# Mixture of experts on three lanes: the third lane starts with expert 1, and the first lane continues behind it

## The chip, the cores and the metric

One core of one Trainium2 chip runs the whole kernel. The metric is the device time of one execution in microseconds (us), the median of several runs. Engines: PE is TensorE, DVE VectorE, ACT ScalarE, POOL GpSimd, SP SyncE, which issues most of the DMAs.

## The reference

One layer over 512 tokens of 1024 channels in float32: a token mixer (not touched here), then a mixture of 16 SwiGLU experts, then a final norm. The router picks two experts of one group of four for each token.

```python
scores = sigmoid(hf @ w_router); sel = scores + router_bias
g_idx = argmax(top_k(sel by groups of 4, 2).sum(-1)); loc = top_k(in_grp, 2)
for e in range(16):
    a = silu(hf @ w_gate[e]) * (hf @ w_up[e])      # 1024 -> 512
    y = y + comb[:, e:e+1] * (a @ w_down[e])       # 512 -> 1024
```

An expert has three matrices of 2 MB each, so 6 MB.

## The kernel before

**Jobs.** Behind the mixer, PE computes the router's logits, and DVE works out the routing in a chain of small operations on tile `rt`. For every expert the tokens that chose it are cut into jobs of up to 64 tokens, at least one job for each expert. The jobs are numbered in the order of the experts: `start[e]` is the first job of expert e, `njobs` their number, and `n_rounds` = njobs/3, rounded up. DVE writes a table `jobs_i` (the expert of each place in each lane), raises `s_jb`, and a little later a table of token indices, `idx_g` and `idx_s`.

**Lanes and rounds.** A round runs three jobs, one in each lane, and each lane has its own buffer for the weights of one expert, in six chunks of 1 MB (`ew<lane>_<chunk>`: 0 and 1 gate, 2 and 3 up, 4 and 5 down). Lane 0 goes from job 0 upwards, lane 1 from the last job downwards, and lane 2 upwards from job `n_rounds`. The executed job j is that of lane j mod 3 in round j div 3. For job j PE does gate(j), up(j), the transposes of the tokens of job j+1 (`tokens`), and down(j-1), which so comes one job late. POOL gathers a job's tokens from `h2_dram` with an indirect DMA and scatters its results.

**Loads.** SP issues the loads. Expert 0 (lane 0) and expert 15 (lane 1) are loaded before the routing is known. Then SP waits for `s_xs`, `s_lg` (logits done) and `s_jb`, reads the expert of lane 2's first job from the table, and loads it. After that it runs a loop over the rounds from 1. Each turn reads six entries of the table, and issues in this order: lane 0 gate and up, lane 1 gate and up, lane 0 down, lane 2 gate and up, lane 1 down, lane 2 down. Each issue waits until the lane's last job has used that chunk (`s_gt`, `s_up`, `s_dn`). Where a lane keeps its expert, the load is still issued, but of 16 columns only (`part_` = 16, 8 KB in place of 1 MB), so that the count of the semaphore `s_er` is the same.

The counts of tokens that the reference's router gives for the 16 experts on these inputs are 43, 93, 57, 63, 195, 68, 139, 128, 5, 29, 23, 37, 30, 10, 40 and 64. That makes 1, 2, 1, 1, 4, 2, 3, 2 jobs for experts 0 to 7, one for each of the others, 24 jobs and 8 rounds. The experts by round are, before the change:

| lane | round 0 | 1 | 2 | 3 | 4 | 5 | 6 | 7 |
|---|---|---|---|---|---|---|---|---|
| 0 | 0 | 1 | 1 | 2 | 3 | 4 | 4 | 4 |
| 1 | 15 | 14 | 13 | 12 | 11 | 10 | 9 | 8 |
| 2 | 4 | 5 | 5 | 6 | 6 | 6 | 7 | 7 |

ACT, during the same stretch, writes the normed tokens to `h2_dram` with four DMAs of its own (L1022), each ahead of a copy of transposed tokens (L1016) for the logits.

Of the kernel before, what the change touches and what calls it, by code (L numbers as in the profile page):

```python
# [30 lines left out]
ALU = mybir.AluOpType  # L31
AX = mybir.AxisListType

P = 128
# [20 lines left out]
MAXR = 11  # L55
# [37 lines left out]
def trunk_kernel(nc, xT, x, cols, consts, masks, w_ada, b_ada_row, w_in, w_o_hgrn, w_o_conv,  # L93
# [15 lines left out]
    with ctx:  # L109
# [105 lines left out]
        rt = at("rt", "ON0", [P, 32, TT * NE])  # L215
# [230 lines left out]
        @block.sync  # L446
        def _(sp):
            sp.dma_start(cols_t[:, :], cols).then_inc(s_par, 16)
            sp.dma_start(con_t[:, :], consts).then_inc(s_par, 16)
            xTv = xT.rearrange("(k p) t -> p k t", p=P)  # L450
            wa = w_ada[0].rearrange("(k p) n -> p k n", p=P)

            def ada_first(b):
                for h in range(2):
                    i, c0 = 2 * b + h, D * (b % 2) + T * (b // 2)
                    sp.dma_start(ada_w[i][:, :, :], wa[:, 4 * h:4 * h + 4, c0:c0 + T]).then_inc(s_ada[i], 16)

            def chunk_load(n):
                sp.dma_start(chunk_view(w_raw, n), chunk_source(n)).then_inc(s_raw[n % 2], 16)

            for h in range(2):
                sp.dma_start(xt_t[:, 4 * h:4 * h + 4, :], xTv[:, 4 * h:4 * h + 4, :]).then_inc(s_xt[h], 16)
            ada_first(0)
            chunk_load(0)
            ada_first(1)
            chunk_load(1)
            ada_first(2)
            ada_first(3)
            sp.dma_start(mask_t[:, :], masks).then_inc(s_par2, 16)
            for n in range(NCH):  # L470
                if n >= 2:
                    sp.wait_ge(s_lo, n - 1)
                    chunk_load(n)
                if n == gn - 1:
                    sp.wait_ge(s_az, 1)
                    sp.dma_start(ada_acc[0:1, :, :].rearrange("p a n -> p (a n)"), b_ada_row).then_inc(s_ab, 16)
                if chunks[n] == ("wo", 1):
                    sp.wait_ge(s_ml, KT)
                    sp.dma_start(gffn[:, :], g_ffn.broadcast_to([P, D])).then_inc(s_gf, 16)
                if chunks[n] == ("wo", 2):  # L480
                    tile_ready(sp, at_step[("ga", 7)])
                    expert_load(sp, 0, 0, 0)
                    expert_load(sp, 0, 0, 1)
                if chunks[n] == ("wo", 0):
                    chunk_used(sp, n - 1)
                    sp.dma_start(x2_t[:, :, :], x.rearrange("(a p) d -> p a d", p=P)).then_inc(s_x, 16)

            expert_load(sp, 0, 0, 2)
            expert_load(sp, 0, 0, 3)
            sp.wait_ge(s_lo, NCH)  # L490
            expert_load(sp, 0, 0, 4)
            expert_load(sp, 0, 0, 5)
            sp.wait_ge(s_ar, 2)
            sp.wait_ge(s_aa, 16 * 8)
            for c in range(3):
                expert_load(sp, NE - 1, 1, c)
            tile_ready(sp, len(steps) - 1)
            for c in range(3, 6):
                expert_load(sp, NE - 1, 1, c)
            sp.wait_ge(s_xs, 4 * TT)  # L500
            sp.wait_ge(s_lg, 1)
            sp.wait_ge(s_jb, 1)
            e2 = sp.value_load(jobs_i[0:1, 2 * MAXR:2 * MAXR + 1], min_val=0, max_val=NE - 1)
            for c in range(6):
                expert_load(sp, e2, 2, c)
            last = last_round(sp)

            with sp.Fori(1, last + 1) as r:
                now = [sp.value_load(jobs_i[0:1, bass.ds(r + MAXR * s, 1)], min_val=0, max_val=NE - 1) for s in range(LANES)]
                old = [sp.value_load(jobs_i[0:1, bass.ds(r + (MAXR * s - 1), 1)], min_val=0, max_val=NE - 1) for s in range(LANES)]  # L510

                for s, cs in ((0, (0, 1, 2, 3)), (1, (0, 1, 2, 3)), (0, (4, 5)), (2, (0, 1, 2, 3)), (1, (4, 5)), (2, (4, 5))):
                    with sp.If(now[s] == old[s]):
                        for c in cs:
                            sp.wait_ge(s_gt if c < 2 else s_up if c < 4 else s_dn, r * LANES + (s - LANES + 1))
                            expert_load(sp, now[s], s, c, 16)
                    with sp.Else():
                        for c in cs:
                            sp.wait_ge(s_gt if c < 2 else s_up if c < 4 else s_dn, r * LANES + (s - LANES + 1))
                            expert_load(sp, now[s], s, c)  # L520

            sp.wait_ge(s_ys, last * (16 * LANES) + (16 * LANES + 16))
            for tt in range(TT):
                sp.dma_start(fin[tt][:, :, :], y_dram.rearrange("(c a p) d -> a p c d", c=2, p=P)[tt]).then_inc(s_fl[tt], 16)
            for tt in range(TT):
                sp.wait_ge(s_fo, tt + 1)
                sp.dma_start(out[P * tt:P * (tt + 1), :], fin[tt][:, 0, :]).then_inc(s_out, 16)
            sp.wait_ge(s_out, 16 * TT)
# [3 lines left out]
        def _(pe):  # L532
# [220 lines left out]
            for t2 in range(TT - 1):  # L753
                for tt in range(t2 + 1, TT):
                    pe.matmul(pp[:, 576 + NE * tt:576 + NE * tt + NE], ones, chosen[:, NE * t2:NE * t2 + NE],
                              start=False, stop=(t2 == TT - 2))
# [17 lines left out]
                mm.then_inc(s_xp, 1)  # L774

            def ff_half(r, s, c, out_ps):
                pe.wait_ge(s_er[s][c], r * 16 + 16)
                w = expert_view(s, c)
                for k in range(4):
                    kb = 4 * (c % 2) + k  # L780
                    j_, c_ = kb // (KT // GT), kb % (KT // GT)
                    for i in range(GT):
                        mm = pe.matmul(out_ps[JS * i:JS * i + JS, 0:FG], heT[:, c_, JS * j_:JS * j_ + JS],  # L783
                                       w[:, k, FG * i:FG * i + FG], start=(kb == 0), stop=(kb == KT - 1))
                return mm
# [22 lines left out]
            def down(j, r, s, first=False):  # L808
                pe.wait_ge(s_at, j + 1)
                if not first:  # L810
                    pe.wait_ge(s_y, j)
                for c in (4, 5):
                    pe.wait_ge(s_er[s][c], r * 16 + 16)
                    w = expert_view(s, c)
                    for k in range(2):
                        fb = 2 * (c - 4) + k
                        i_, c_ = fb // (4 // GT), fb % (4 // GT)
                        for i in range(GT):
                            mm = pe.matmul(ha[JS * i:JS * i + JS, 1, 0:DG_], aT[:, c_, JS * i_:JS * i_ + JS],  # L819
                                           w[:, k, DG_ * i:DG_ * i + DG_], start=(fb == 0), stop=(fb == 3))  # L820
                mm.then_inc(s_dn, 1)
# [245 lines left out]
        def _(dve):  # L1067
# [308 lines left out]
            def go(ins):  # L1376
                n_r[0] += 1
                ins.then_inc(s_r, 1)

            def settle():  # L1380
                dve.wait_ge(s_r, n_r[0])

            def r(i, a=0, b=TT * NE):
                return rt[:, i, a:b]
# [7 lines left out]
            def tt_(o, a, b, op):  # L1392
                go(dve.tensor_tensor(o, a, b, op))
# [92 lines left out]
            io = con_t[:, K_IO:K_IO + P]  # L1486
            steps_r = io[:, 0:MAXR]
            njobs = incl[:, NE - 1:NE]
            n_rounds, behind, left = r(27, 0, 1), r(27, 1, 2), r(27, 2, 3)
            ids = rt[:, 28, 0:NPOS]  # L1490
            ide = rt[:, 29, 0:NPOS]
            off_ = rt[:, 30, 0:MAXR]
            lane_ = lambda ap, s: ap[:, MAXR * s:MAXR * (s + 1)]
            tt_(start, incl, nb, ALU.subtract)
            tt_(rt[:, 25:27, :], twice(slot), rt[:, 13:15, :], ALU.mult)
            go(dve.scalar_tensor_tensor(off_, steps_r, 3.0, njobs.broadcast_to([P, MAXR]), ALU.mult, ALU.is_lt))
            go(dve.tensor_scalar(behind, njobs, -1.0, None, ALU.add))
            go(dve.tensor_copy(lane_(ids, 0), steps_r))
            settle()
            start_b = start.rearrange("p (o e) -> p o e", o=1)  # L1500
            tt_(by_tt(job), by_tt(div), start_b.broadcast_to([P, TT, NE]), ALU.add)
# [2 lines left out]
            go(dve.scalar_tensor_tensor(lane_(ids, 1), steps_r, -1.0, behind.broadcast_to([P, MAXR]), ALU.mult, ALU.add))  # L1504
            settle()
            tt_(rt[:, 15:17, :], twice(job), rt[:, 13:15, :], ALU.mult)
            tt_(left, njobs, n_rounds, ALU.subtract)
            go(dve.tensor_scalar(lane_(ids, 2), steps_r, n_rounds, None, ALU.add))
            for c in range(2 * TT):
                dve.tensor_scalar(slot1[:, c, :].rearrange("p (g s) -> p g s", g=GT),  # L1510
                                  io[:, 0:JS].rearrange("p (o s) -> p o s", o=1).broadcast_to([P, GT, JS]),
# [1 line left out]
                                  ALU.is_equal, ALU.mult).then_inc(s_oh1, 1)  # L1513
            settle()
            go(dve.tensor_reduce(r(18, 8, 16), rt[:, 15:17, :].rearrange("p c (a e) -> p (c a) e", e=NE), AX.X, ALU.add))
            go(dve.tensor_copy(ide, ids))
            go(dve.scalar_tensor_tensor(off_, lane_(ids, 2), 1.0, left.broadcast_to([P, MAXR]), ALU.mult, ALU.is_ge))
            settle()
            go(dve.scalar_tensor_tensor(lane_(ids, 2), off_, 64.0, lane_(ids, 2), ALU.mult, ALU.add))
            tt_(lane_(ide, 2), lane_(ide, 2), off_, ALU.subtract)  # L1520
            settle()
            tt_(job1[:, :, :], ids.rearrange("p (o j) -> p o j", o=1).broadcast_to([P, 2 * TT, NPOS]),
                col(r(18, 8, 16)).broadcast_to([P, 2 * TT, NPOS]), ALU.is_equal)
# [239 lines left out]
```

## Time and profile before

| | us |
|---|---|
| median of 3 runs | 964.48 (962.88 to 972.04) |
| profiled execution, its own time | 964.68 |
| span of its trace | 962.8 |
| PE busy in the span | 854.4 |
| routing and first gather, last logits matmul to first token transpose | about 609.6 to 638.5 |
| the 24 jobs, first gate matmul to last down matmul | 640.3 to 934.4 |

Times in the trace are us from the start of the span. The profiled execution is 0.2 us from the median, so its stretches can be used as they are. A matmul line names the source line: L783 is gate and up, L819 down, L773 the token transposes, L437 the DMA issue of an expert's chunk.

### The profile page before, as it was taken

To read this page: it belongs to the slowest core of one execution; us is meant where nothing else is said; L and a number is where in the kernel's file an instruction comes from. 1 tells how busy PE (TensorE), PEld (TensorE's weight loads), DVE (VectorE), ACT (ScalarE), POOL (GpSimd) and SP (SyncE) were. 2 spreads that over 40 slices of the span, in tenths; PEclk is the share of its full clock that TensorE was granted. 3 is DMA by queue.
4 is the path that set the end of the run, shared out by engine and by line. 5 is a ranking of instruction groups with operands and counts; after the bars stand their busy time and mean duration, and the time that the engine had idled before them with its cause. 6 is when DMAs were issued, how large, how long until landed. Compare 5 with 4: busy or idle time off the path is not lost.

```text
span 962.8 us, 13420 instructions
## 1 busy us (share of the span) xinstructions
PE 854.4 (89%) x5250; PEld 628.0 (65%) x5250; DVE 499.1 (52%) x667; ACT 205.2 (21%) x258; POOL 216.7 (23%) x218
## 2 busy tenths in 40 slices
PE   2699999999999999888999898459999979999970
PEld 0378889988799877666888697445555534555530
DVE  2533797996789965868989556411111101111116
ACT  4332211212331134521223233101000000000012
POOL 0100312121623200233444330012222212222220
PEclk9999999999989999988999999769999989999995
DMA  9903221212121211157776839389998999999716
GB/s 317 330 4 128 88 88 58 75 45 88 44 89 44 66 66 44 44 165 229 241 244 201 291 138 332 128 312 390 399 348 303 393 396 393 393 364 393 267 44 261
DMA packets 119436, 198.44 MB, mean 206 GB/s; under 512 B 10567, under 2 KB 64087, under 8 KB 119393
## 3 DMA queue, kind: packets, MB, share of 16 engines
q1 hardware_dynamic: 97746, 167.43, 48.3%
q10 hardware_dynamic: 17616, 19.40, 6.2%
q0 software_dynamic: 4032, 11.03, 3.1%
q8 instruction: 29, 0.48, 0.2%
q14 instruction: 13, 0.11, 0.0%
HBM read 189.44 MB, written 10.49 MB: 208 GB/s over the span
## 4 chain that ended last, share of the span: by engine, by line
PE 64%; DVE 13%; DMA 9%; SPq 7%; issue 4%; ACT 2%; POOL 1%; ACTq 0%; DVEq 0%; POOLq 0%
PE proj L783 14%; PE proj L535 9%; PE proj L537 9%; PE proj L536 9%; PE ha L819 7%; SPq L437 5%; DMA ada_p<-in_w_ada 5%; PE pp L610 5%; DVE ada_acc L1337 4%; DVE osq L1313 2%; DMA ew<-in_w_down 2%; DVE tmp L1194 1%; DMA ada_w<-in_w_ada 1%; PE pp L773 1%; PE ha L671 1%
## 5 line engine op out<-in xcount | busy, mean ns | idle before, releaser
L783 PE MATMUL proj<-ew,heT 128*64 128x256 f32 x1536 | 178.9, 386 | 8.0 <-DMA ew<-in_w_gate 5.8
L783 PEld LDWEIGHTS proj<-ew,heT 128*64 128x64 f32 x1536 | 109.5, 139 | 76.4 <-issue 18.9
L535 PE MATMUL proj<-h_hi,w_hi 128*128 128x512 f32 x368 | 148.1, 402 | 8.9 <-DVE h_lo L1133 6.5
L537 PE MATMUL proj<-h_hi,w_lo 128*128 128x512 f32 x368 | 144.1, 392 | 0.0
L536 PE MATMUL proj<-h_lo,w_hi 128*128 128x512 f32 x368 | 144.0, 391 | 0.0
L1629 POOL TENSOR_TENSOR w_lo<-w_raw,w_hi 128x2048 fp32r<-128x2048 f32 x16 | 77.5, 4843 | 128.4 <-ACT w_hi L865 128.4
L819 PE MATMUL ha<-ew,aT 128*64 128x512 f32 x384 | 88.1, 599 | 3.4 <-DMA ew<-in_w_down 2.4
L865 ACT ACTIVATE w_hi<-w_raw 128x2048 fp32r<-128x2048 f32 x38 | 72.5, 1908 | 79.0 <-PE proj L537 35.0
L1242 DVE SCALAR_TENSOR_TENSOR acc<-u_t,cols_t,acc 128x512 f32<-128x512 f32 x120 | 87.8, 793 | 0.0
L535 PEld LDWEIGHTS proj<-h_hi,w_hi 128*128 128x128 f32 x368 | 69.6, 189 | 27.6 <-issue 8.2
L537 PEld LDWEIGHTS proj<-h_hi,w_lo 128*128 128x128 f32 x368 | 69.5, 189 | 14.9
L536 PEld LDWEIGHTS proj<-h_lo,w_hi 128*128 128x128 f32 x368 | 69.7, 190 | 14.4 <-issue 1.0
L1337 DVE SCALAR_TENSOR_TENSOR ada_acc<-ada_p,cact,ada_acc 128x256 f32<-128x256 f32 x128 | 66.3, 590 | 8.1 <-DMA ada_p<-in_w_ada 8.1
L1569 DVE TENSOR_TENSOR y_sb<-ha,rows 128x512 f32<-128x512 f32 x24 | 16.6, 691 | 93.9 <-PE ha L819 93.9
L1094 DVE TENSOR_TENSOR w_lo<-w_raw,w_hi 128x2048 fp32r<-128x2048 f32 x22 | 52.8, 2401 | 20.3 <-ACT w_hi L865 20.3
L1558 DVE TENSOR_TENSOR a_t<-proj,sg_t 128x256 f32<-128x256 f32 x24 | 10.2, 425 | 93.8 <-PE proj L783 93.8
L819 PEld LDWEIGHTS ha<-ew,aT 128*64 128x64 f32 x384 | 25.5, 136 | 49.2 <-issue 45.9
L1564 DVE COPY aT<-ha 128x256 f32<-128x256 f32 x24 | 10.2, 425 | 79.8 <-PE ha L805 79.8
L1672 POOL COPY gi<-idx_g 128x1 int32 (+1 forms) x26 | 4.9, 188 | 204.9 <-PE pp L773 153.4
L610 PEld LDWEIGHTS pp<-q_t,k_t 128*128 128x128 f32 (+3 forms) x448 | 45.6, 178 | 1.2 <-issue 0.7
L610 PE MATMUL pp<-q_t,k_t 128*128 128x64 f32 (+3 forms) x448 | 45.9, 260 | 0.0
L1034 ACT ACTIVATE sg_t<-proj 128x256 f32<-128x256 f32 x24 | 9.2, 384 | 162.1 <-PE proj L783 162.1
(227 smaller groups left out, 1328.6 us busy)
## 6 DMA issues: line engine op xcount, KB each, us to landing
ew<-in_w_gate SPq DMA_DIRECT2D x34, 1024.0 KB, 12.7
ew<-in_w_up SPq DMA_DIRECT2D x34, 1024.0 KB, 14.3
ew<-in_w_down SPq DMA_DIRECT2D x34, 1024.0 KB, 14.3
w_raw<-in_w_in SPq DMA_DIRECT2D x28, 1024.0 KB, 5.1
ada_p<-in_w_ada ACTq DMA_DIRECT2D x32, 512.0 KB, 5.2
ada_w<-in_w_ada SPq DMA_DIRECT2D x8, 1024.0 KB, 13.5
w_raw<-in_w_o_hgrn SPq DMA_DIRECT2D x4, 1024.0 KB, 5.0
w_raw<-in_w_out SPq DMA_DIRECT2D x4, 1024.0 KB, 7.9
```

Source lines behind the costliest of these rows:

```text
L437: eng.dma_start(dst, src).then_inc(s_er[s][c], 16)
L535: pe.matmul(outap, a_hi, b_hi, start=first, stop=False)
L536: pe.matmul(outap, a_hi, b_lo, start=False, stop=False)
L537: return pe.matmul(outap, a_lo, b_hi, start=False, stop=last)
L610: mm = pe.matmul(pp[0:keys, 64 * u:64 * u + 64], k_t[:, h, P * c:P * c + keys], tblk(q_t[:, h, P * c:P * c + P], m, 1), start=True, stop=True)
L783: mm = pe.matmul(out_ps[JS * i:JS * i + JS, 0:FG], heT[:, c_, JS * j_:JS * j_ + JS], w[:, k, FG * i:FG * i + FG], start=(kb == 0), stop=(k ...
L819: mm = pe.matmul(ha[JS * i:JS * i + JS, 1, 0:DG_], aT[:, c_, JS * i_:JS * i_ + JS], w[:, k, DG_ * i:DG_ * i + DG_], start=(fb == 0), stop= ...
L865: act.activation(w_hi[:, n % 2, :], w_raw[:, n % 2, :], ACT.Copy).then_inc(s_hi, 1)
L1094: dve.tensor_tensor(w_lo[:, n % 2, :], w_raw[:, n % 2, :], w_hi[:, n % 2, :].bitcast(F32), ALU.subtract).then_inc(s_lo, 1)
L1242: dve.scalar_tensor_tensor(acc[:, ct, :], src, tap, acc[:, ct, :], ALU.mult, ALU.add).then_inc(s_cv, 1)
L1337: dve.scalar_tensor_tensor(dst, ada_p[pc][:, kk, :], cact[:, kk:kk + 1], dst, ALU.mult, ALU.add).then_inc(s_aa, 1)
L1629: pool.tensor_tensor(w_lo[:, n % 2, :], w_raw[:, n % 2, :], w_hi[:, n % 2, :].bitcast(F32), ALU.subtract).then_inc(s_lo, 1)
```

## The change

SP loads expert 1 into lane 2 without waiting for the routing: chunks 0 to 3 when the squares of x2 are done (`s_xs`), chunks 4 and 5 when the logits are done (`s_lg`), as their buffers are free only then. It then waits for all six to land, waits for the table, and issues a load of 16 columns if lane 2's first expert is 1, or the whole expert if not. PE's waits for lane 2's chunks count 16 more.

The jobs are dealt out in another way. With `third` = njobs - 2 n_rounds and `first` = min(n_rounds, start[1]), lane 2 begins at job `first`, the first job of expert 1; lane 0 runs the first `first` jobs and goes on with those behind lane 2's last. Lane 1 is as before. DVE computes this with some other small operations.

```diff
             sp.wait_ge(s_xs, 4 * TT)
+            for c in range(4):
+                expert_load(sp, 1, 2, c)
             sp.wait_ge(s_lg, 1)
+            for c in (4, 5):
+                expert_load(sp, 1, 2, c)
+            for c in range(6):
+                sp.wait_ge(s_er[2][c], 16)
             sp.wait_ge(s_jb, 1)
             e2 = sp.value_load(jobs_i[0:1, 2 * MAXR:2 * MAXR + 1], min_val=0, max_val=NE - 1)
-            for c in range(6):
-                expert_load(sp, e2, 2, c)
+            with sp.If(e2 == 1):
+                for c in range(6):
+                    expert_load(sp, e2, 2, c, 16)
+            with sp.Else():
+                for c in range(6):
+                    expert_load(sp, e2, 2, c)
...
             def ff_half(r, s, c, out_ps):
-                pe.wait_ge(s_er[s][c], r * 16 + 16)
+                pe.wait_ge(s_er[s][c], r * 16 + (32 if s == 2 else 16))
...
-            n_rounds, behind, left = r(27, 0, 1), r(27, 1, 2), r(27, 2, 3)
+            n_rounds, behind, third, first = [r(27, a, a + 1) for a in range(4)]
...
-            go(dve.tensor_copy(lane_(ids, 0), steps_r))
...
-            tt_(left, njobs, n_rounds, ALU.subtract)
-            go(dve.tensor_scalar(lane_(ids, 2), steps_r, n_rounds, None, ALU.add))
+            go(dve.scalar_tensor_tensor(third, n_rounds, -2.0, njobs, ALU.mult, ALU.add))
+            tt_(first, n_rounds, start[:, 1:2], ALU.min)
...
-            go(dve.tensor_copy(ide, ids))
-            go(dve.scalar_tensor_tensor(off_, lane_(ids, 2), 1.0, left.broadcast_to([P, MAXR]), ALU.mult, ALU.is_ge))
+            go(dve.tensor_scalar(lane_(ids, 2), steps_r, first, None, ALU.add))
+            go(dve.scalar_tensor_tensor(off_, steps_r, 1.0, third.broadcast_to([P, MAXR]), ALU.mult, ALU.is_ge))
+            go(dve.tensor_scalar(skip, steps_r, first, third, ALU.is_ge, ALU.mult))
+            settle()
+            tt_(lane_(ide, 2), lane_(ids, 2), off_, ALU.subtract)
+            tt_(lane_(ids, 0), steps_r, skip, ALU.add)
             settle()
             go(dve.scalar_tensor_tensor(lane_(ids, 2), off_, 64.0, lane_(ids, 2), ALU.mult, ALU.add))
-            tt_(lane_(ide, 2), lane_(ide, 2), off_, ALU.subtract)
+            go(dve.tensor_copy(ide[:, 0:2 * MAXR], ids[:, 0:2 * MAXR]))
```

## Rows read from the trace of the kernel before

**Rows 1.** the page: the span, and part 6 (DMA issues, whole chunks)

```profile
span 962.8 us, 13420 instructions
...
ew<-in_w_gate SPq DMA_DIRECT2D x34, 1024.0 KB, 12.7
```

**Rows 2.** view of the DMA, issues of 8 KB

```profile
ew<-in_w_gate SPq DMA_DIRECT2D x14, 8.0 KB, 11.2
```

**Rows 3.** busy time by stretch: engines, TensorE clock, DMA share, GB/s

```profile
595.00:610.00 15.00, 12.80 (x96) 10.88 (x96) 5.05 (x5) 6.17 (x8) 0.00 (x0) 0.89 0.97 359
610.00:625.00 15.00, 4.09 (x20) 3.81 (x20) 10.76 (x67) 1.71 (x3) 0.00 (x0) 0.62 0.01 4
625.00:630.00 5.00, 3.60 (x16) 3.49 (x16) 2.73 (x12) 0.00 (x0) 0.00 (x0) 0.50 0.06 7
630.00:640.00 10.00, 1.12 (x4) 0.72 (x4) 0.72 (x3) 0.34 (x1) 1.80 (x5) 0.50 0.98 355
...
720.00:730.00 10.00, 10.00 (x82) 5.61 (x79) 1.54 (x3) 0.98 (x2) 2.04 (x5) 1.00 0.33 120
730.00:770.00 40.00, 40.00 (x300) 21.26 (x296) 5.32 (x10) 2.94 (x6) 10.35 (x22) 1.00 1.04 391
```

**Rows 4.** timeline of PE, jobs: start us, us, instruction [idle before]

```profile
650.65 3.67 PE L783 MATMUL proj<-ew,heT 128*64 128x256 f32 x32 [0.69 <-ACT heT L1040]
...
766.69 3.62 PE L783 MATMUL proj<-ew,heT 128*64 128x256 f32 x32
...
784.26 5.32 PE L783 MATMUL proj<-ew,heT 128*64 128x256 f32 x32 [5.80 <-DMA ew<-in_w_gate]
...
792.70 1.95 PE L783 MATMUL proj<-ew,heT 128*64 128x256 f32 x16 [0.67 <-DMA ew<-in_w_up]
...
917.67 3.62 PE L783 MATMUL proj<-ew,heT 128*64 128x256 f32 x32
```

**Rows 5.** waits of PE, 636 to 940 us: us in total, times, longest

```profile
PE ha L819 <- DMA ew<-in_w_down: 2.4, 4, 0.7
```

**Rows 6.** timeline of SP, the issues of expert loads

```profile
592.74 1.02 SPq L437 DMA_DIRECT2D ew<-in_w_down  x2
628.66 1.37 SPq L437 DMA_DIRECT2D ew<-in_w_gate  x2
...
726.46 0.96 SPq L437 DMA_DIRECT2D ew<-in_w_gate  x2
...
729.26 4.82 SPq L437 DMA_DIRECT2D ew<-in_w_gate  x2
...
757.76 6.73 SPq L437 DMA_DIRECT2D ew<-in_w_down  x4
769.18 2.90 SPq L437 DMA_DIRECT2D ew<-in_w_gate  x2
```

**Rows 7.** tile xg at 629 to 640 us, the first gather

```profile
DMA to landing us min/median/max: 7.1/7.1/7.1
```

**Rows 8.** tile xg at 900 to 930 us, the last gathers

```profile
DMA to landing us min/median/max: 3.1/3.4/3.9
```

**Rows 9.** timeline of ACT at 595 to 612 us

```profile
595.24 1.28 ACT L859 ACT_TABLE_LOAD   x1
...
596.79 0.35 ACTq L1022 DMA_DIRECT2D h_rows<-h_t  x1
598.82 1.02 ACT L1016 ACTIVATE h2T<-ha 128x1024 f32<-128x1024 f32 x1 [2.08 <-PE ha L726]
...
610.25 1.28 ACT L859 ACT_TABLE_LOAD   x1
```

**Rows 10.** timeline of DVE, last steps of the routing

```profile
624.49 0.28 DVE L1515 TENSOR_REDUCE rt<-rt 128x8 f32<-128x128 f32 x1
...
624.97 0.17 DVE L1519 SCALAR_TENSOR_TENSOR rt<-rt 128x11 f32<-128x11 f32 x1
...
625.25 0.43 DVE L1393 TENSOR_TENSOR job<-rt 128x264 f32<-128x264 f32 x1
```

More of the change, by code:

```diff
@@ L812, in down @@
                 for c in (4, 5):
-                    pe.wait_ge(s_er[s][c], r * 16 + 16)
+                    pe.wait_ge(s_er[s][c], r * 16 + (32 if s == 2 else 16))
                     w = expert_view(s, c)
@@ L1492, in _ @@
             off_ = rt[:, 30, 0:MAXR]
+            skip = rt[:, 31, 0:MAXR]
             lane_ = lambda ap, s: ap[:, MAXR * s:MAXR * (s + 1)]
```

## The prediction

> **What bounds the kernel now.** I read the page first [rows 1, 2]: 34 whole issues for the gate matrices, two for each expert, so 17 experts are loaded whole for 16 experts, and 14 issues of 8 KB, so 7 times a lane keeps its expert. That agrees with the table of rounds: seven repeats in it, and expert 4 twice, in lane 2 and again in lane 0. Next come stretches around the change [rows 3]. DMA is full from 595 to 610, at 0.01 from 610 to 625 and at 0.06 from 625 to 630, while the routing is worked out on small DVE operations, and full again from 630 on, by the load of expert 4 that waited for the table. From 720 to 730 it is at 0.33, then full again. So the routing leaves nearly 20 us of DMA unused, and the loop then asks for it back.
>
> Then PE's jobs [rows 4]. From the gate of job 1 (650.65) to that of job 11 (766.69) ten jobs take 116.04, so 11.60 a job, back to back: here PE is the bound, and what DMA does can't be seen. From job 11 to job 23 (917.67) twelve jobs take 150.98, against 12 x 11.60 = 139.2. The 11.8 us between are what late weights cost: 5.80 and 0.67 of waiting at job 12, a gate there of 5.32 in place of 3.62 (the clock had fallen), and 2.4 in four waits for down matrices [rows 4, 5], the rest being what the engine loses around such waits. So the end is set by PE plus 11.8 us of DMA, and one gather at the beginning, 7.1 us, for which everything waits [rows 7].
>
> **What the change does to the loads.** By the counts, `start[1]` = 1, so `first` = 1 and `third` = 8. The lanes become 0 5 5 6 6 6 7 7; 15 14 13 12 11 10 9 8; and 1 1 2 3 4 4 4 4. All experts are loaded once: 16 whole loads, of which 13 are in the loop (14 before), by round 2, 2, 3, 2, 1, 2, 1 against 3, 1, 3, 2, 2, 2, 1. The page of after should show 32 whole issues and 18 small ones for each matrix: 7 repeats become 8, and lane 2's first place makes nine.
>
> **The load moved into the routing.** SP passes `s_xs` at about 595. Data still to come then is 15 us x 359 GB/s = 5.4 MB by 610 [rows 3]; with expert 1's 6.3 MB that is 11.7 MB, at the 391 GB/s of a full stretch 30 us, so it lands at 625 to 627. SP's new wait for the six chunks is over before or about when `s_jb` comes (SP issued at 628.66 [rows 6]), and what is queued behind it on SP, six small loads and the turn for round 1, has slack, for that turn waits until job 0's gate is done at about 645. Job 2 needs lane 2 only at 662. If that cover were gone, each us of lateness past 645 would delay round 1's loads, which have a few us of slack themselves. I cost it at nothing.
>
> **The gather.** The first gather was issued at 631.39 beside expert 4's load and took 7.1 [rows 7]; the last ones, on a quiet DMA, took 3.1 to 3.9, median 3.4 [rows 8]. With expert 4's load gone, only the six small loads lie beside it. It gains 3.7 (bounds 0, if expert 1 is still landing, and 4.0). PE, ACT and POOL all wait for it, so it counts in full.
>
> **The routing's arithmetic.** The stages before `job1` took 0.48 us (three operations) and 0.28 us (two) [rows 10], so one more operation is 0.08 and one more stage 0.28. After there are four, two and two operations, so +0.36, less 0.16 for one copy and one scalar operation taken out of the stages before: +0.2, on the path. `s_jb` is later by the same, with slack on SP.
>
> **The loop.** A turn of SP starts some 4.7 us after the last issue of the turn before (757.76 + 6.73 to 769.18 [rows 6]), and this last issue waits for a down of PE, so turns are tied to PE's pace. Round 1 has two loads in place of three, behind no load of expert 4: no wait. Round 2 has two in place of one. Lane 2's down chunks are its last issue, at about 721.5, some 5 us ahead of round 3's first issue (726.46 [rows 6]); at 2.8 us a chunk ((792.70 - 784.26)/3 [rows 4]) they are nearly through, and round 3 begins with at most 1 us of backlog. I take 0.5.
>
> Round 3 is three whole loads in both kernels, 18 chunks on a queue that is served in order. Before, the 19th chunk, the first of job 12, landed when the gate began, at 784.26, 5.97 us after it was due (766.69 + 11.60 = 778.29). After, job 12 keeps expert 6, and its chunks are small. But they are issued behind the 18, and PE waits for them all the same: small issues landed after a median of 11.2 us [rows 2]. So they land one chunk earlier than before, at 784.26 - 2.8 = 781.5, and the gate still waits 3.2 us. Whether 3.2 us of idling lowers the clock is open: after 5.8 us it cost 5.32 - 3.62 = 1.7; after waits of 0.7 it cost nothing [rows 4]. I take half, 0.8. Left at job 12: 3.2 + 0.5 + 0.8 = 4.5.
>
> Behind it, round 4 needs 12 whole chunks from 781.5, 5.7 us a pair: job 13's gate lands at 787, its up at 793, job 14's gate and up at 799 and 804.5, the downs at 810 and 816. PE asks for them at 793, 797, 805, 809, 813 and 824.5: none late. Job 15's small chunks come at 816.3 and are due at 816.4, so nothing or some tenths. From round 5 on there are 1, 2 and 1 loads in rounds of 34.8 us, which at 17 us a load DMA has to spare. So the loop gives 11.8 - 4.5 = 7.3 (bounds 11.8 if no wait is left, and 2.9 in the rival below).
>
> **Sum.** -7.3 - 3.7 + 0.2 = -10.8 us. The profiled execution took 964.68, 0.2 from the median: 953.9 us.
>
> **Rivals.** (1) The waits vanish wholly: the small chunks are not held up, as their bytes are few. Against it stand the 11.2 us they took before. Gain 11.8 + 3.7 - 0.2 = 15.3, time 949.4.
>
> (2) DMA stays the bound behind job 12: the clock falls fully (1.7), round 3 starts 1 us later, and the waits for job 13's to job 16's weights (11.8 - 5.97 - 2.8 = 3.0) stay. Left are 3.2 + 1.7 + 1.0 + 3.0 = 8.9, so the loop gives 2.9: 964.68 - 2.9 - 3.5 = 958.3.
>
> (3) ACT is held up by SP's issues. ACT issues its write of `h2` at 596.79 in 0.35 us and copies for the logits at 598.82 [rows 9], when SP had finished issuing (592.74 + 1.02) and was waiting. After, SP issues four chunks from 595 on behind three that are in flight. In round 3 SP issued four quickly, and the next two took 4.82 [rows 6]: some five chunks in flight, then it waits for one to land. So SP would sit in its issue for one chunk, some 3 us, about 597 to 600. If ACT can't issue meanwhile, its first copy and all of the routing come up to 3 us later, less 1.7 of its slack at best: I price it at +2.5, time 956.4. No row of before has ACT issuing in such a time, so the bounds are 0 and 3, and further chunks wait on `s_lg`.
>
> The Trainium skill (Perfetto Trace Analysis, DMA Instruction — HWDGE) says that the generator of descriptors is one block, locked by one issuing engine for as long as it generates, and that another waits for the lock; it titles the section for DVE and Sync and notes that the pair in use is SP and ACT. By that this rival holds and the time is that of (3); by the rows at 596.79 and 598.82 alone nothing would be seen.
>
> (4) Slower: instructions or tables that engines fetch over DMA during the routing. At 610 to 625 DMA was at 0.01, and would be full. A fetch behind full queues could lose what the gather lost, 7.1 - 3.4 = 3.7 us. With three on the path of DVE or PE that is 11.1, more than the 10.8 gained, so 965.0 and slower from the third fetch on. Against it: ACT's table load took 1.28 us at 595.24 with DMA full and 1.28 at 610.25 with DMA idle [rows 9], and the dense stretch at 595 to 610 had DMA full too [rows 3].
>
> (5) The change doesn't do what it says: if expert 0 had filled lane 0, `e2` would not be 1, and a seventeenth load would come after the table, with nothing gained: 964.9.
>
> **How the numbers follow.** Chances: forecast 0.47, (1) 0.10, (2) 0.15, (3) 0.22, (4) 0.04, (5) 0.02. The range is 950 to 961: it holds the forecast with its bounds, (2) and (3), and leaves out most of (1), (4) and (5). A measurement of this kernel tells about 1% from no change, here 9.6 us, a time of 954.8; my forecast lies 0.9 below it. Faster by over 1%: three quarters of the forecast, all of (1), a fifth of (3) and of (2)'s lower edge little: 0.50. Within 1%: 0.47. Slower by over 1%, 974 and more, only if (4) is worse than priced: 0.03.
>
> **What would show it.** The page of after: 32 whole and 18 small issues of each matrix. DMA full from 595 to about 625. The first gather 3.1 to 4 us, the first gate at about 636.8. Ten jobs or more at 11.60. One wait at job 12 of 3 to 4 us, released by a load of 16 columns, and none above 1 us behind it. ACT's issue at about 597: 0.35, or some 3 us by (3). Idle time in DVE's chain at 610 to 628 would show (4). The prediction is wrong if round 3 starts late, if the queue isn't served in order, or if the stretch up to the logits grows.

## The result and the profile after

The changed kernel takes 961.91 us (median of 20 runs, 958.01 to 968.99), the kernel before in the same series 968.64 (20 runs). The ratio is 0.995, with a 95% interval of 0.993 to 0.997: faster by about 4.8 us, a small difference but clear of the noise, and less than half of the 10.8 forecast. The two medians by themselves lie 6.7 us apart. The profiled execution has a span of 957.1, against 962.8, so 5.7 less. The page, its span and the whole chunks [rows 1]:

```profile
span 957.1 us, 13441 instructions
...
ew<-in_w_gate SPq DMA_DIRECT2D x32, 1024.0 KB
```

The view of the DMA, its issues of 8 KB [rows 2]:

```profile
ew<-in_w_gate SPq DMA_DIRECT2D x18, 8.0 KB
```

32 and 18, as counted: 16 whole loads. Next the stretches of [rows 3] (busy time of PE, PEld, DVE, ACT, POOL, then TensorE's granted clock, DMA share, GB/s):

```profile
595.00:610.00 15.00, 13.07 (x99) 11.13 (x100) 4.79 (x4) 6.08 (x8) 0.00 (x0) 0.89 1.01 388
610.00:625.00 15.00, 3.90 (x20) 3.62 (x19) 11.19 (x70) 1.26 (x2) 0.00 (x0) 0.61 1.01 385
625.00:630.00 5.00, 3.60 (x16) 3.49 (x16) 2.73 (x12) 0.00 (x0) 0.00 (x0) 0.50 0.04 12
630.00:640.00 10.00, 4.46 (x20) 2.67 (x22) 0.64 (x3) 0.60 (x1) 2.94 (x6) 0.50 0.23 57
...
720.00:730.00 10.00, 10.00 (x74) 5.28 (x74) 1.54 (x3) 0.98 (x2) 1.77 (x5) 1.00 1.03 404
730.00:770.00 40.00, 38.85 (x294) 20.81 (x290) 5.05 (x10) 3.32 (x7) 9.41 (x19) 1.00 1.05 391
```

From 610 to 625 DMA is at 1.01 and was at 0.01; just behind 625 it falls to almost nothing, so expert 1 has landed. From 630 to 640 it is almost idle, where expert 4's load was. From 720 to 730, where it was at 0.33, it is now full, and that is where the forecast went wrong. The timeline of PE, the jobs [rows 4]:

```profile
634.86 1.12 PE L783 MATMUL pp<-con_t,xg 128*128 128x128 f32 x4 [5.39 <-DMA xg<-h_rows,gi]
636.66 8.99 PE L793 MATMUL proj<-ew,heT 128*64 128x256 f32 x64 [0.69 <-ACT heT L1050]
...
646.92 3.67 PE L793 MATMUL proj<-ew,heT 128*64 128x256 f32 x32 [0.69 <-ACT heT L1050]
...
762.97 3.63 PE L793 MATMUL proj<-ew,heT 128*64 128x256 f32 x32
...
768.12 1.95 PE L793 MATMUL proj<-ew,heT 128*64 128x256 f32 x16 [1.15 <-DMA ew<-in_w_up]
771.30 1.95 PE L793 MATMUL proj<-ew,heT 128*64 128x256 f32 x16 [1.24 <-DMA ew<-in_w_up]
...
776.42 1.94 PE L829 MATMUL ha<-ew,aT 128*64 128x512 f32 x8 [0.53 <-DMA ew<-in_w_down]
782.57 5.96 PE L793 MATMUL proj<-ew,heT 128*64 128x256 f32 x32 [4.22 <-DMA ew<-in_w_gate]
...
796.50 3.62 PE L793 MATMUL proj<-ew,heT 128*64 128x256 f32 x32
...
912.50 3.62 PE L793 MATMUL proj<-ew,heT 128*64 128x256 f32 x32
```

The tokens of job 0 come 5.39 us after PE began to wait (8.96 before). Ten jobs take 116.05 from 646.92 to 762.97, 11.60 each as before. From the gate of job 11 to that of job 23 it is 149.5, against 139.2 for twelve jobs; over all 22 jobs from job 1 on, 10.4 us of late weights are left of 11.8. They sit elsewhere: 1.15 and 1.24 at job 11's up, 0.53 at job 10's down, 4.22 at job 12, whose gate then takes 5.96 in place of 3.62, at a mean granted clock of 0.61; behind it there is none. The timeline of SP (chunk pairs; start, time in the issue):

```profile
687.89 0.85 SPq L437 DMA_DIRECT2D ew<-in_w_gate  x2
...
690.29 0.95 SPq L437 DMA_DIRECT2D ew<-in_w_gate  x2
...
697.18 4.44 SPq L437 DMA_DIRECT2D ew<-in_w_gate  x2
...
706.60 11.25 SPq L437 DMA_DIRECT2D ew<-in_w_down  x4
722.57 0.93 SPq L437 DMA_DIRECT2D ew<-in_w_gate  x2
723.61 5.78 SPq L437 DMA_DIRECT2D ew<-in_w_up  x2
...
770.65 0.88 SPq L437 DMA_DIRECT2D ew<-in_w_gate  x2
```

Round 2's first whole chunks are issued at 690.29, behind two pairs of small ones at 687.89. Round 3 begins at 722.57, 17.6 us into job 6 as before (17.8), but its second pair takes 5.78 to issue where it took 1.30: the queue is full already. Job 12's small chunks, issued from 770.65 on, land at 782.57, 60.0 us after round 3's first issue. Before, it was 57.8 us, with one whole chunk more.

The 5.7 us between the two spans split so, each from a row at either end (the scores' first DVE operation at 610.81 and 610.34, the first gather's issue at 631.39 and 631.30, the first gate at 640.31 and 636.66, the second at 650.65 and 646.92, the last at 917.67 and 912.50):

| stretch | before | after | difference |
|---|---|---|---|
| start to scores (not touched) | 610.81 | 610.34 | -0.5 |
| scores to the gather's issue | 20.58 | 20.96 | +0.4 |
| gather's issue to first gate | 8.92 | 5.36 | -3.6 |
| first gate to second gate | 10.34 | 10.26 | -0.1 |
| late weights, second gate to last (over 22 x 11.60) | 11.8 | 10.4 | -1.4 |
| last gate to end (not touched) | 45.1 | 44.6 | -0.5 |

### The profile page after: what moved, and what is told of

It is laid out like the page before. It is cut to its first block, busy times and chain, and to the rows that moved or that the text cites. A ratio compares the mean times of both kernels' runs of the same rounds, so it can differ in the third digit from the quotient of the medians.

```text
span 957.1 us, 13441 instructions
## 1 busy us (share of the span) xinstructions
PE 852.7 (89%) x5250; PEld 627.5 (66%) x5250; DVE 500.0 (52%) x669; ACT 205.1 (21%) x258; POOL 216.6 (23%) x218
## 4 chain that ended last, share of the span: by engine, by line
PE 70%; DVE 11%; DMA 7%; SPq 5%; issue 4%; ACT 2%; POOL 1%; ACTq 0%; DVEq 0%; POOLq 0%
PE proj L793 16%; PE proj L545 11%; PE proj L546 10%; PE proj L547 10%; PE ha L829 7%; PE pp L620 5%; DMA ada_p<-in_w_ada 3%; SPq L437 3%; DVE ada_acc L1347 2%; DVE osq L1323 2%; PE pp L783 1%; DMA ada_w<-in_w_ada 1%; DMA ew<-in_w_gate 1%; DVE tmp L1204 1%; PE ha L681 1%
## 5 line engine op out<-in xcount | busy, mean ns | idle before, releaser
L1583 DVE TENSOR_TENSOR y_sb<-ha,rows 128x512 f32<-128x512 f32 x24 | 16.6, 692 | 91.8 <-PE ha L829 91.8
```

## The experiments

The mixer ahead of the routing varies by up to 15 us between profiled executions, so spans of single executions say little about a few us. I read the stretches of the table instead. "Late weights" always means the time from job 1's gate to job 23's, less 22 x 11.60 = 255.2. Ratios are to the kernel before on the same chip. Time before the first gate is counted from the issue of the first gather.

| kernel | ratio (95%) | gather to first gate | late weights | longest wait for weights |
|---|---|---|---|---|
| before | | 8.9 | 11.8 | job 12, 5.80 |
| after | 0.995 (0.993 to 0.997) | 5.4 | 10.4 | job 12, 4.22 |
| new dealing alone | 0.998 (0.995 to 1.000) | 8.3 | 10.6 | job 12, 4.22 |
| load during the routing alone | 0.997 (0.995 to 1.000) | 5.4 | 11.8 | job 12, 5.79 |
| after, no small loads | 0.986 (0.982 to 0.989) | 5.3 | 1.5 | 0.45 |
| after, late down chunks | 0.985 (0.980 to 0.989) | 5.4 | 0.05 | none |
| before, no small loads | 1.000 (0.997 to 1.004) | 8.4 | 10.6 | job 12, 5.18 |
| after, both | 0.984 (0.978 to 0.989) | 5.2 | 0.05 | none |
| before, late down chunks | 0.994 (0.990 to 0.997) | 8.3 | 4.8 | job 13, 1.24 |
| before, gather first | 1.003 (1.000 to 1.007) | 5.2 | 17.6 | jobs 6 and 12, 3.75 and 5.97 |
| after, turns written out | one run | 5.2 | 8.5 | job 12, 4.26 |
| the same, one load less | one run | 5.3 | 4.2 | job 12, 2.06 |
| the same, job 6 without small loads | one run | 5.2 | 6.7 | job 12, 4.26 |
| the same, job 12 without small loads | one run | 5.2 | 10.6 | job 15, 4.25 |

**Each half of the change alone.** First the dealing, with lane 2's first expert loaded after the table:

```diff
-            for c in range(4):
-                expert_load(sp, 1, 2, c)
             sp.wait_ge(s_lg, 1)
...
             sp.wait_ge(s_jb, 1)
             e2 = sp.value_load(...)
...
+            for c in range(6):
+                expert_load(sp, e2, 2, c)
```

> Only the new dealing of the jobs: lane 2's first expert (1) is loaded after the table, as before the change. My theory: the changed kernel lost its gain because its whole loads of jobs 7 to 11 lie in one run, which begins at 690.3 us and ends at job 12. Expert 1's load beside the first gather doesn't touch that run. So the 24 jobs keep the 10.4 us of late weights of the changed kernel (11.8 before the change), job 12 again waits some 4 us for a small load, and the first gather is back at about 7 us. Profiled span about 961.5, ratio to the kernel before 0.999. Rival (the deal itself pays or costs more, and the load moved into the routing hides it): the late weights differ from 10.4 by over 2 us, and the span is under 959 or over 964.

Late weights came to 10.6, job 12 waited 4.22, and the gather took its old time. Then the load during the routing, with the old dealing, so of expert 4:

```diff
             sp.wait_ge(s_xs, 4 * TT)
+            for c in range(4):
+                expert_load(sp, 4, 2, c)
             sp.wait_ge(s_lg, 1)
+            for c in (4, 5):
+                expert_load(sp, 4, 2, c)
```

> The old dealing of the jobs, but lane 2's first expert, which is 4 in it, is loaded during the routing. Theory: this gives the gather's 3.6 us and nothing in the jobs, since round 3's run begins at 726 us behind an idle DMA: 11.8 us of late weights stay. Profiled span about 959.3, ratio 0.996. Rival (one load less ahead of round 1 also relieves the later rounds): late weights under 10 us, span under 957.5.

Timeline of PE in this kernel, job 0's tokens and job 12's gate:

```profile
634.61 1.11 PE L783 MATMUL pp<-con_t,xg 128*128 128x128 f32 x4 [5.45 <-DMA xg<-h_rows,gi]
...
781.12 5.71 PE L793 MATMUL proj<-ew,heT 128*64 128x256 f32 x32 [5.79 <-DMA ew<-in_w_gate]
```

5.45 ahead of the tokens, as in the changed kernel, and 5.79 at job 12, as before. Late weights 11.8. So by the stretches the two halves add up without touching each other: about 3.6 us from the gather, 1.4 or 1.2 from the dealing. The whole times alone wouldn't show it, as the interval of either half reaches to 1.000. Over all the kernels here the stretch ahead of the first gate is 8.3 to 8.9 us with a load beside the gather and 5.2 to 5.4 without, so the gather's share is 2.9 to 3.7.

**Where the dealing's gain went.** In this kernel a lane that keeps its expert issues no DMA in the loop:

```diff
                     with sp.If(now[s] == old[s]):
                         for c in cs:
                             sp.wait_ge(...)
-                            expert_load(sp, now[s], s, c, 16)
+                            sp.nop().then_inc(s_er[s][c], 16)
```

> The changed kernel, where a lane that keeps its expert raises the semaphore from SP itself, with no DMA of 16 columns in the loop. Theory: job 12's weights are in its buffer already, and it waited only because its small load stood behind the whole loads of round 3. Its wait of 4.2 us and the 2.3 us of lowered clock go; the waits of job 11's up matrices (2.4) and job 10's down (0.5) stay, for the run of loads is as long. Late weights 10.4 - 6.5 = 3.9 us or a little less, span about 950.6, ratio 0.987. Rival (DMA throughput is what binds, and the queue's order doesn't matter): the wait moves to job 13 or 14, late weights stay at 8 us or more, span over 955.

All waits for weights that its timeline of PE shows:

```profile
774.85 1.94 PE L829 MATMUL ha<-ew,aT 128*64 128x512 f32 x8 [0.35 <-DMA ew<-in_w_down]
...
810.32 1.94 PE L829 MATMUL ha<-ew,aT 128*64 128x512 f32 x8 [0.45 <-DMA ew<-in_w_down]
```

1.5 us are left, less than the 3.9 expected: not only job 12's wait is gone, but job 11's too, for round 2's first whole chunks came 2.4 us earlier, with no small issues ahead of them. The next kernel keeps the small loads and changes SP's order:

```diff
+            def turn(r, tail):
...
+                part_load(0, (0, 1, 2, 3), now[0], old[0], free(0))
+                if tail:
+                    part_load(2, (4, 5), old[2], entry(r + (MAXR * 2 - 2)), r * LANES + (2 - 2 * LANES + 1))
+                part_load(1, (0, 1, 2, 3), now[1], old[1], free(1))
+                part_load(0, (4, 5), now[0], old[0], free(0))
+                part_load(2, (0, 1, 2, 3), now[2], old[2], free(2))
+                part_load(1, (4, 5), now[1], old[1], free(1))
```

> The changed kernel, where SP issues the down chunks of lane 2 of a round behind lane 0's gate and up chunks of the next round, so that a turn no longer waits for them; small loads are kept. Theory: round 2's whole loads can start at about 685.5 and not 690.3, round 3's at about 711 and not 722.6; at 2.95 us a chunk job 11's up lands at 761, job 12's small chunks at about 767, before 774.6, when they are due. No late weights at all: span 957.1 - 10.4 = 946.7, ratio 0.983. Rival (the run of five loads is simply too long for DMA): it starts at most 4.8 us earlier, so job 12 still waits about 3 us with its loss of clock, and 5 us or more of late weights stay, span over 951.

Its timeline of SP, the first whole pair of round 2, its last one, and the first of round 3:

```profile
684.02 0.95 SPq L437 DMA_DIRECT2D ew<-in_w_gate  x2
...
703.77 0.93 SPq L437 DMA_DIRECT2D ew<-in_w_down  x2
709.58 0.93 SPq L437 DMA_DIRECT2D ew<-in_w_gate  x2
```

Round 3 begins at 709.6, 6.2 us into job 6 and not 17.6. DMA in this kernel (clock, share, GB/s):

```profile
680.00:690.00 10.00, 1.00 0.58 211
690.00:700.00 10.00, 1.00 1.05 385
```

and in the changed kernel:

```profile
680.00:690.00 10.00, 1.00 0.21 62
690.00:700.00 10.00, 1.00 0.84 273
```

The idle time at 680 to 690, at 0.21, lay in front of a run of five whole loads that ended at job 12. It is filled to 0.58, and no wait is left. The 13 loads of the loop were never too many; they were asked for too late.

**Which of the two is at work in the kernel before.**

```diff
-                            expert_load(sp, now[s], s, c, 16)
+                            sp.nop().then_inc(s_er[s][c], 16)
```

> The kernel before, with the loop's small loads replaced by an increment of the semaphore from SP. Theory: small loads cost where PE waits for one behind whole loads, and where they hold up the first whole load of a round behind an idle DMA. In the old dealing job 12 changes its expert, so its 5.8 us wait is for a whole load and stays; late weights 11 to 11.8 us, span about 962.5, ratio 1.000. Rival (small loads cost DMA time in themselves, so that taking them out helps any kernel, as it gave the changed one 9 us): late weights under 9 us, span under 960.

10.6 us, 1.3 less than before and just under what I expected, ratio 1.000: small loads matter little where job 12's load is a whole one. Then both edits in the changed kernel:

> The changed kernel with lane 2's down chunks issued late and without small loads. Theory: with the late issue alone nothing of the late weights was left (0 us), so there is nothing more to gain: the 24 jobs at 11.60 each, span within 1.5 us of 945.3, ratio 0.984. Rival (DMA traffic beside PE costs something even without waits): span under 943.5.

As expected: 0.05 us, gates 11.60 apart, and nothing more. The spans (945.3 and 947.6) differ by what lies ahead of the routing. Then the new order in the kernel before:

> The kernel before, old dealing and expert 4 loaded after the table, with only the order on SP changed: lane 2's down chunks behind lane 0's gate and up of the next round. Theory: the queue's order was the bound, more than the count of loads. From 628.7 on DMA runs through; at 2.95 us a chunk job 12's gate lands at about 776 before it is due at 778.3, its up and job 13's within 1 to 3 us of their due times. Late weights 1 to 3 us in place of 11.8, the first gather as before: span about 953, ratio 0.990. Rival (17 loads after the table are too many for the DMA, and only the change's freed load makes the new order work): late weights over 6 us, span over 957.

4.8 us are left, above the 1 to 3 expected and under the rival's 6: the order alone takes away 7.0 of 11.8. The rest can't come from an idle queue: in this kernel the share of DMA is 1.01 or more in every stretch of 4 us from 638 to 818. Here the DMA's own pace is the bound, and only fewer loads behind the table can help, as the change has them. Whether its dealing or its load during the routing gives that was not run apart. Given the right order, the change is worth about 2.9 us at the gather (8.3 to 5.4) and 4.8 at the weights, 0.985 against 0.994, more than in the order it was made in.

**The gather.** The kernel before, where expert 4's load waits for the first gather:

```diff
             e2 = sp.value_load(...)
+            sp.wait_ge(s_g, 16)
             for c in range(6):
                 expert_load(sp, e2, 2, c)
```

> The kernel before, where SP also waits for the first gather to land before it loads expert 4. Theory: the gain ahead of the jobs came only from a first gather with nothing beside it. It lands in 3.3 to 3.9 us in place of 7.1, the first gate begins 3.5 us earlier, and the 6 MB asked for 6 us later still land before job 2 (662 us) and before round 3. Late weights stay 11.8; span about 959.3, ratio 0.996, the same as with expert 4 loaded during the routing. Rival (the load moved into the routing was needed for that gain): rounds 1 or 2 show new waits and the span is 961 or more.

The gather was as fast as expected, so its contention is shown. But the kernel is no faster than before (1.003), and my theory failed on the second half; the rival, new waits in rounds 1 or 2, came true. Its timeline of PE has a wait that none of the others has, and its timeline of SP the issue that PE waited for:

```profile
693.39 3.62 PE L784 MATMUL proj<-ew,heT 128*64 128x256 f32 x32
...
708.91 5.36 PE L784 MATMUL proj<-ew,heT 128*64 128x256 f32 x32 [3.75 <-DMA ew<-in_w_gate]
```

```profile
695.12 0.87 SPq L437 DMA_DIRECT2D ew<-in_w_gate  x2
```

693.39 is the gate of job 5, 708.91 that of job 6. Job 6 keeps expert 1 in lane 0, so its weights were in the buffer already. What PE waited for is again a pair of small loads, issued at 695.12 and landed 13.7 us later, behind the 24 whole chunks of expert 4 and round 1. That run begins 5.6 us later than before (634.21 and 628.66) and PE comes 3.7 us earlier (job 1 at 646.95 and 650.65), which is more than the slack that the run had. Job 6 is 3.9 us past due, and with the lowered clock it costs 5.7; with job 12 as before, late weights are 17.6. In this queue the load during the routing pays for the gather. Whether it would still be needed if a lane that keeps its expert raised its semaphore from SP is not tested.

**The step of the prediction that failed, by itself.** The last four have a single run each (965.1, 954.0, 956.0 and 966.4 us in the order of the table, 968.0 for the kernel before), so only their traces are used. All have turns 1 to 4 of SP's loop written out one by one, with constants in place of the loop's register; the first has nothing else.

> A control for the three beside it: the changed kernel with turns 1 to 4 of SP's loop written out, nothing else. Theory: the same waits as in the changed kernel, late weights about 10.4 us. Rival (registers and the loop's head made the turns late): under 9 us.

8.5 us: the theory missed and the rival's under 9 came true. Written out, the turns begin about 1 us earlier (round 3 at 16.6 us into job 6 in place of 17.6), and late weights are 1.8 us less. 0.9 of that is in job 12's gate, which takes 5.11 and not 5.96 behind the same wait; such a difference comes by itself (see the clock below), so the 1 us of queue gave about 1 us. This kernel is the control for the next three.

```diff
-            turn(2, {})
+            turn(2, {2: 'force'})
```

The diff is against the control; `'force'` gives job 8 loads of 16 columns, so what it computes is not the layer's.

> As the control, but job 8 (lane 2 in round 2) loads only 16 columns of each chunk and computes with the weights of expert 1 that lie there: the weights of expert 2 are left out. So round 3's three loads begin with an empty queue, as the prediction had it. Theory: the prediction's step failed by this backlog alone. Job 11 then waits for nothing, job 12's small load lands 18 chunks of 2.95 us and 1.6 us after round 3's first issue, which is 2.7 us past due, and with a part of the lowered clock the late weights are 3 to 5 us. Rival (the prediction was wrong about the queue in another way, for one in its speed): over 6 us, or none.

Its timeline of SP at the beginning of round 3, and of PE at jobs 11 and 12:

```profile
722.91 0.96 SPq L437 DMA_DIRECT2D ew<-in_w_gate  x2
723.96 1.27 SPq L437 DMA_DIRECT2D ew<-in_w_up  x2
```

```profile
764.28 3.62 PE L807 MATMUL proj<-ew,heT 128*64 128x256 f32 x32
...
778.11 5.36 PE L807 MATMUL proj<-ew,heT 128*64 128x256 f32 x32 [2.06 <-DMA ew<-in_w_gate]
```

The second pair is issued in 1.27 us: an empty queue. DMA just ahead of that first issue (clock, share, GB/s) was almost idle in this kernel, and full in the changed kernel:

```profile
718.00:722.00 4.00, 1.00 0.20 62
```

```profile
718.00:722.00 4.00, 1.00 1.03 406
```

Job 12's gate begins at 778.11, 55.2 us after round 3's first issue, where it was 60.0 in the changed kernel and in the control; it is 2.2 us past due, and nothing else waits. Late weights 4.2, where the prediction had 4.5.

```diff
-            turn(2, {})
+            turn(2, {0: 'inc'})
```

With `'inc'` a lane that keeps its expert runs `sp.nop().then_inc(s_er[s][c], 16)` in place of the small load; in turn 2 and lane 0 that is job 6.

> As the control, but job 6 (lane 0 in round 2) keeps its weights with no small loads, the semaphore raised from SP itself. Theory: the first whole load of round 2 is issued 2.4 us earlier (1.8 us of two pairs of small issues and the gap between), and all behind it in the run lands as much earlier: no wait over 0.3 us for job 11's up, but job 12 still waits behind the queue; late weights 10.4 - 2.4 = 8.0 us, 7.2 to 8.8. Rival (small loads hurt only where PE waits for them): 10 us or more stay.

Round 2's first issue is now that of whole chunks:

```profile
688.28 0.98 SPq L437 DMA_DIRECT2D ew<-in_w_gate  x2
```

That is 17.6 us into job 3, against 19.2 in the control, and late weights fall from 8.5 to 6.7 (expected 8.0 from 10.4): by 1.8 for 1.6 us, in single runs whose clocks differ too (job 12's gate 5.36 and 5.11). As expected, job 11's up no longer waits and job 12 still does, 4.26. The same edit for job 12 alone, in turn 4:

> As the control, but job 12 (lane 0 in round 4) keeps its weights with no small loads. Theory: the run is as long as before and job 11's up matrices come as late (waits of 1.15 and 1.24) and job 10's down by 0.5, but job 12 doesn't wait, and the clock doesn't fall: late weights 3.5 to 4.2 us. Rival (the DMA's throughput binds): job 13 waits in its place, 6 us or more.

```profile
784.85 3.62 PE L807 MATMUL proj<-ew,heT 128*64 128x256 f32 x32
...
816.85 1.94 PE L843 MATMUL ha<-ew,aT 128*64 128x512 f32 x8 [0.61 <-DMA ew<-in_w_down]
819.32 1.94 PE L843 MATMUL ha<-ew,aT 128*64 128x512 f32 x8 [0.53 <-DMA ew<-in_w_down]
825.50 4.80 PE L807 MATMUL proj<-ew,heT 128*64 128x256 f32 x28 [4.25 <-DMA ew<-in_w_gate]
```

Here my theory failed. Job 12 doesn't wait, job 11 does as expected, but 10.6 us stay, and the rival's job 13 is not their place either. Job 15, the next that keeps its weights in lane 0, waits 4.25 for its small load, with its gate at a lowered clock (0.70 on the mean, 5.23 for all 32 matmuls), and jobs 13 and 14 don't wait for their gate or up matrices. The 0.61 and 0.53 are at job 13's down. The prediction had job 15's small chunks due at 816.4 and landing at 816.3: with no slack there, what PE no longer lost at job 12 it lost at job 15. So job 12's small load alone isn't the cause: each lane that keeps its expert asks at the end of the queue, and the next one waits instead.

## Why the prediction was wrong

**What held.** The counts of loads; expert 1 landed just behind 625 (forecast 625 to 627) and held up nothing. The gather and what follows it gave 3.6 (3.7). No wait behind job 12. The place and kind of the main wait, job 12's small chunks behind round 3's 18, were as forecast.

**What failed: round 3's backlog.** The step "round 3 begins with at most 1 us of backlog. I take 0.5" is the one. Its 18 chunks and the small ones behind them landed 60.0 us after the first issue; with the empty queue of the kernel with one load less it was 55.2. So the backlog was 4.8 us. The bytes agree: of the 12 chunks (12.6 MB) that SP had asked for from 690.29 on, its queue had moved 10.46 MB by 722.57 (view of the DMA in that window), so two chunks were still to come. I had judged it from the last issue of round 2 alone, as if the queue were empty when that was made, and had not followed the queue from the round's first whole chunk. That one is issued at 690.29, 20.1 us into job 3, since two small pairs and their gap come first, and 12 chunks from there end at 726 to 728, not at 723 as the 0.5 had it. (An estimate: 2.98 us a chunk, (55.2 - 1.6)/18, where 1.6 is what small loads took alone late in the kernel before.) The prediction itself, in rival (3), counted some five chunks in flight where SP is held in its issue, and didn't use that here. The 0.5 us should have been 4.8.

**The clock at job 12, a smaller error.** I took 0.8. It was 5.96 - 3.62 = 2.3 behind 4.22 us of waiting, and 5.36 - 3.62 = 1.7 behind only 2.06. It doesn't follow the length of the wait: behind 4.22 to 4.26 us at job 12 the gate took 5.11, 5.36, 5.96 and 6.60 in four kernels, so 1.5 to 3.0 more, and what decides between them stays open. With 3.2 + 4.8 + 2.3 = 10.3 the sum of the prediction gives the 10.4 measured. The 3.2 + 4.8 are how late job 12's gate begins; part of that is lost at job 11's up and job 10's down already, so job 12's own wait is only 4.22.

**The routing's arithmetic** cost 0.4, not 0.2 (20.96 to 20.99 us from the scores to the gather's issue in each kernel with the new dealing, 20.57 to 20.58 in those with the old). The stages ahead of `job` took 1.30 us in place of 0.76, so 0.54 more where the sum had 0.36.

**The rivals.** (2) came nearest, with 8.9 us of late weights, but for other reasons: 1 us of backlog and waits at jobs 13 to 16 that didn't come. That its 958.3 lies beside the 958.97 of the profiled execution is luck. (1) and (5) didn't happen. Nor did (4): with the old dealing and the load during the routing, the scores to the gather's issue took 20.58 us, as before the change, though DMA was full. (3) is refuted by a timeline that the kernel before did not have. ACT's issues in the changed kernel:

```profile
596.23 0.35 ACTq L1032 DMA_DIRECT2D h_rows<-h_t  x1
598.26 1.03 ACT L1026 ACTIVATE h2T<-ha 128x1024 f32<-128x1024 f32 x1 [2.08 <-PE ha L736]
598.27 0.34 ACTq L1032 DMA_DIRECT2D h_rows<-h_t  x1
...
599.83 0.33 ACTq L1032 DMA_DIRECT2D h_rows<-h_t  x1
...
602.71 0.33 ACTq L1032 DMA_DIRECT2D h_rows<-h_t  x1
```

and SP at that time, a single issue:

```profile
595.23 8.71 SPq L437 DMA_DIRECT2D ew<-in_w_up  x1
```

SP sat in one issue from 595.23 to 603.94, and ACT issued four DMAs in that time at 0.33 to 0.35 each. The Trainium skill (Perfetto Trace Analysis, DMA Instruction — HWDGE) has one generator, locked by the engine that uses it; an ACT that waits for that lock isn't seen here, and the measurement decides. Whether SP held the lock in all of its 8.71 us, no run shows.

**Size.** The forecast of -10.8 against -4.8 measured: 5.9 us of the difference are the late weights (10.4 for 4.5), the rest small terms. The time of 961.91 lies 8.0 above the 953.9 forecast; 2.9 of that is the distance of this kernel's median from its profiled execution (958.97). The forecast had started from an execution 0.2 from the median of three runs; over 20 runs that median is 968.64.

## What to carry to other kernels

A load taken out of a full queue gains only if it is taken out of the run of loads that ends at the wait, and then only what that run was behind: here a whole load less, some 18 us of queue, took late weights from 8.5 to 4.2. Follow that run back to its first issue and ask what held that up: here a wait for PE, a 4.7 us turn of the loop (717.85 to 722.57 ahead of round 3) and four small DMAs in front. Issuing the chunks that come free last behind those that are needed first took away all 10.4 us, after a change of the dealing that had saved a whole load had taken 1.4. And a DMA that moves next to nothing still comes behind what was issued before it: the 8 KB that job 6 waited for in the kernel with the gather first took 13.7 us to land, against 1.6 alone. Keep it out of a queue of megabytes.

## What the runs showed of the hardware

Three things. First, a TensorE that idled for 2.06 us ran its next 32 matmuls in 5.36 us in place of 3.62, at a mean granted clock of 0.68, so a wait shorter than the 3.75 to 5.97 us of the other cases was enough; waits of 0.3 to 1.35 us cost no clock. Second, an engine's DMA issues took 0.33 to 0.35 us each while another engine sat 8.71 us in its own. Third, job 12 waited 4.22, 4.22, 4.26 and 4.26 us in four kernels in which its queue was late by different amounts, and job 15 4.25 in a fifth. What fits all five: the down matrices of the job before last, which came just late in each (0.29 to 0.53 us of waiting), stand two whole chunks ahead of the small ones in the queue. So PE is at the queue's pace there, and the wait is the time between the two landings, 6.15 us in the changed kernel (776.42 to 782.57), less the 1.94 of the matmuls between.
